# VectorE takes more low parts, the sums of squares end in one buffer, and norms, residual scaling and top-k rounds change places in a three-layer fp32 kernel

## The reference, cut to what matters

```python
def first_block(x, ...):
    x = x + _gla_mixer(_rmsnorm(x, gla_norm), ...)   # head norms, silu(z), w_out
    x = x + _s5_mixer(_rmsnorm(x, s5_norm), ...)
    return _rmsnorm(x, final_norm)

def _s5_mixer(h, ...):
    u, z = jnp.split(h @ w_in, [D_INNER], axis=-1)
    # b_bar from lam, dt and b; states by an associative scan; y = Re(states c) + d_skip * u
    y = jax.nn.gelu(y)
    y = y * jax.nn.sigmoid(y @ w_glu + b_glu) * jax.nn.silu(z)
    return y @ w_out

def second_block(x, meta_tokens, ...):
    h = h + hybrid_mixer(rmsnorm(h, attn_norm_g), pos, topk, ...)
    h = h + swiglu(rmsnorm(h, ffn_norm_g), ...)
    return rmsnorm(h, final_norm_g)[:, N_META:t]

# in hybrid_mixer, for blocks of 128 queries (topk = 128):
    logits = einsum('bqhd,bkd->bqhk', q_idx, k_idx) * idx_scale
    score = einsum('bqh,bqhk->bqk', w_idx, relu(logits))     # index scores
    _, sel = lax.top_k(where(causal, score, -inf), topk)     # then attention over the chosen keys
```

## Time and profile before

| | |
|---|---|
| median of 3 runs | 1885.07 us (1885.0 to 1887.94) |
| the profiled execution's own time | 1887.52 us |
| its span | 1885.7 us |
| mean granted TensorE clock | 0.957 |
| TensorE busy | 1752.2 us, 93% |
| VectorE busy | 1011.8 us, 54% |
| ScalarE busy | 689.3 us, 37% |
| GpSimd busy | 640.9 us, 34% |

### The profile page before, as it was taken

The page is one execution under the profiler, slowest core; times in us unless marked ns, Lnnn a source line. Parts: engine busy times, 40 slices in busy tenths (PEclk is TensorE's granted clock), DMA queues, the critical chain, the costliest instruction groups (busy, mean ns, idle before and its releaser), DMA issues.

```text
span 1885.7 us, 22105 instructions
## 1 busy us (share of the span) xinstructions
PE 1752.2 (93%) x8796; PEld 1419.1 (75%) x8796; DVE 1011.8 (54%) x1469; ACT 689.3 (37%) x1040; POOL 640.9 (34%) x227
## 2 busy tenths in 40 slices
PE   4999999999699999898999999998798999999997
PEld 4777677888588888787788877686576878888786
DVE  4046345486678888897365446599853222222001
ACT  4372225433333353534433331423465322232121
POOL 2433002344522222231134423051574344333441
PEclk8999998999899999799999999899899999999998
DMA  4322001333445544354655322121000333332331
GB/s 136 100 69 80 30 5 63 90 89 101 138 106 144 138 123 122 78 134 111 212 195 168 90 66 67 45 62 56 23 1 23 90 89 90 90 102 79 92 93 60
DMA packets 270941, 172.07 MB, mean 91 GB/s; under 512 B 90971, under 2 KB 249782, under 8 KB 270710
## 3 DMA queue, kind: packets, MB, share of 16 engines
q1 hardware_dynamic: 242272, 146.99, 27.7%
q10 hardware_dynamic: 28262, 22.02, 3.9%
q0 software_dynamic: 304, 1.65, 0.3%
HBM read 149.64 MB, written 20.97 MB: 90 GB/s over the span
## 4 chain that ended last, share of the span: by engine, by line
PE 76%; DVE 11%; ACT 5%; DMA 3%; issue 2%; POOL 1%; ACTq 1%; SPq 0%; DVEq 0%; POOLq 0%
PE PS L680 20%; PE PS L682 20%; PE PS L681 20%; DVE acc L2299 2%; PE PA L932 1%; PE PA L931 1%; POOL ring_lo L2426 1%; PE PA L911 1%; DVE top L2298 1%; PE PA L864 1%; PE PS L1202 1%; PE PA L861 1%; PE PS L1190 1%; PE PA L840 1%; DMA ring<-in_s_w_in 1%
## 5 line engine op out<-in xcount | busy, mean ns | idle before, releaser
L2426 POOL TENSOR_TENSOR ring_lo<-ring,ring_hi 128x2048 fp32r<-128x2048 f32 (+4 forms) x102 | 447.6, 4388 | 909.4 <-ACT ring_hi L1305 908.9
L1305 ACT ACTIVATE ring_hi<-ring 128x2048 fp32r<-128x2048 f32 (+2 forms) x123 | 223.8, 1822 | 213.4 <-PE PS L682 163.8
L680 PE MATMUL PS<-U3h,ring_hi 128*128 128x512 f32 x352 | 140.7, 400 | 3.1 <-POOL ring_lo L2426 3.1
L682 PE MATMUL PS<-U3h,ring_lo 128*128 128x512 f32 x352 | 140.0, 398 | 0.0
L681 PE MATMUL PS<-U3l,ring_hi 128*128 128x512 f32 x352 | 138.6, 394 | 0.0
L2464 POOL TENSOR_TENSOR W<-PW,CZ 128x1024 f32<-128x1024 f32 x16 | 34.6, 2160 | 255.6 <-ACT CZ L1482 255.5
L680 PE MATMUL PS<-HT5h,ring_hi 128*128 128x512 f32 x256 | 108.5, 424 | 0.0
L2391 DVE TENSOR_TENSOR SF<-PS,rs 128x512 f32<-128x512 f32 x22 | 15.2, 692 | 166.7 <-PE PS L682 166.6
L681 PE MATMUL PS<-HT5l,ring_hi 128*128 128x512 f32 x256 | 103.3, 403 | 0.0
L682 PE MATMUL PS<-HT5h,ring_lo 128*128 128x512 f32 x256 | 102.9, 402 | 0.0
L2479 POOL TENSOR_SCALAR PB<-PB,mx 128x144 f32<-128x144 f32 (+3 forms) x64 | 71.2, 1125 | 36.2 <-DVE mx L2348 36.2
...
## 6 DMA issues: line engine op xcount, KB each, us to landing
...
```

What stands on the lines that cost most here:

```text
L680: pe.matmul(dst, w[0], x[0], start=start, stop=False)
L682: return pe.matmul(dst, w[1], x[0], start=False, stop=stop)
L1305: act.activation(ring_hi[:, n % NSLOT, 0:plan.size[n]], ring[:, n % NSLOT, 0:plan.size[n]], ACT.Copy)\
L2426: pool.tensor_tensor(ring_lo[:, n % NSLOT, at], ring[:, n % NSLOT, at], ring_hi[:, n % NSLOT, at].bitcast(F32), ALU.subtract).then_inc(wlo ...
```

## The change: what it does

1. VectorE makes the low parts of four more weight loads: the second and third of the S5 stage, and the first two of the second glu half (`DVE_LOADS`).
2. VectorE also adds the last square of a wide norm to `ssq`, and TensorE sums from `ssq` alone.
3. The head norms' sums stand behind one gate tile and their rows behind the next (`HEAD_SUMS`, `HEAD_USE`).
4. At the start of S5 the reciprocal stands before the last step of `b_factors(0)`, `turns(0)` behind the first scaled u tile.
5. In a batch, `c_to_columns` and `columns` stand behind the second transposes of b.
6. The gelus of batch 13 stand in batch 15.
7. The residual scaling stands in pairs 23 to 30.
8. The low parts of the latent queries stand behind all three scalings; one index score stands a step later.
9. Between the rotations there are 32 top-k rounds instead of 40, in the pairs 24 instead of 16.

```diff
@@ -227,8 +227,8 @@
     LOWS = [range(s5_used[b - 1] + 3 if b else S5_LOAD + 3, s5_used[b] + 3) for b in range(NBATCH)]
-    DVE_LOADS = range(LOWS[0].start, LOWS[-1].stop)
-    assert DVE_LOADS.stop <= S5_END
+    DVE_LOADS = range(S5_LOAD + 1, S5_END + 2)
+    assert LOWS[-1].stop <= S5_END
     pairs("s5_glu", wg2[:, GA:], 0, KI)
@@ -576,6 +576,7 @@
         FIRST_MLA = PAIRS.index(("mla", 0, 0))
+        XT_PAIR = len(PAIRS) - KD - 1
@@ -607,7 +608,7 @@
-            return sum(NORMS[other][2] - 2 for other in WIDE[:WIDE.index(name)]) + max(i, 1)
+            return sum(NORMS[other][2] - 1 for other in WIDE[:WIDE.index(name)]) + max(i, 1)
@@ -646,7 +647,10 @@
-        HEAD_WITH = {0: 0, 2: 1, 6: 2, 10: 3}
+
+
+        HEAD_SUMS = {1: 0, 3: 1, 6: 2, 10: 3}
+        HEAD_USE = {0: 0, 4: 1, 8: 2, 12: 3}
@@ -759,15 +763,9 @@
                     norm_applied(pe, BEFORE[name])
-                parts = [sq[:, (s0 + i) % 2, :] for i in range(k)]
-                if name in WIDE:
-                    pe.wait_ge(squares_summed, summed(name, k - 2))
-                    parts = [ssq, parts[-1]]
-                pe.wait_ge(sq_ready, s0 + k)
+                pe.wait_ge(squares_summed, summed(name, k - 1))
                 for j, w in token_tiles(width):
-                    for i, part in enumerate(parts):
-                        m = pe.matmul(PA[0:w, 3, j:j + 1], part[:, j * P:j * P + w], con[:, C_ONE:C_ONE + 1],
-                                      start=i == 0, stop=i == len(parts) - 1)
+                    m = pe.matmul(PA[0:w, 3, j:j + 1], ssq[:, j * P:j * P + w], con[:, C_ONE:C_ONE + 1], start=True, stop=True)
                 m.then_inc(sq_used, k)
@@ -866,8 +864,13 @@
-            pair_stage("gla_z", lambda k: both((HT2h, HT2l), slice(None), k), split="gla2",
-                       then=lambda i: norm(f"head{HEAD_WITH[i]}", T) if i in HEAD_WITH else None)
+            def head_norms(i):
+                if i in HEAD_SUMS:
+                    norm_sums(f"head{HEAD_SUMS[i]}", T)
+                if i - 1 in HEAD_SUMS:
+                    norm_rows(f"head{HEAD_SUMS[i - 1]}", T)
+
+            pair_stage("gla_z", lambda k: both((HT2h, HT2l), slice(None), k), split="gla2", then=head_norms)
             single_stage("gla_out", lambda k: both((Oh, Ol), slice(None), k), split="o")
@@ -948,19 +951,16 @@
                 beside = BESIDE[b]
+                dense(*beside[0], 0, 1)
+                additions(b)
+                dense(*beside[0], 1, 4)
+                if b + 1 < NBATCH:
+                    b_to_rows(b + 1, 0)
+                dense(*beside[0], 4, KD)
+                if b + 1 < NBATCH:
+                    b_to_rows(b + 1, 1)
                 if b + 2 < NBATCH:
                     c_to_columns(b + 2)
-                if beside[0]:
-                    dense(*beside[0], 0, 1)
-                additions(b)
-                if beside[0]:
-                    dense(*beside[0], 1, 4)
-                if b + 1 < NBATCH:
-                    b_to_rows(b + 1, 0)
-                if beside[0]:
-                    dense(*beside[0], 4, KD)
-                if b + 1 < NBATCH:
-                    b_to_rows(b + 1, 1)
                 if len(beside) > 1:
...
@@ -1416,14 +1411,17 @@
             for i, tile in enumerate(tiles["gla_z"]):
-                if i in HEAD_WITH:
-                    h = HEAD_WITH[i]
-                    norm(f"head{h}", lambda k: O[:, 4 * h + k, :], T, GDV)
+                if i + 1 in HEAD_SUMS:
+                    h = HEAD_SUMS[i + 1]
+                    for k in range(4):
+                        square(f"head{h}", k, O[:, 4 * h + k, :], T)
                 split_weights(tile.loads[-1] + 1)
                 if i >= 2:
                     act.wait_ge(val_ready, VALS["o"] + i - 1)
                 act.wait_ge(tile_done, tile.t + 1)
                 act.activation(SZ[:, i % 2, :], PS[:, 2 * tile.slot, :], ACT.Silu).then_inc(slot_free[tile.slot], 1)
+                if i in HEAD_SUMS:
+                    std(f"head{HEAD_SUMS[i]}", T, GDV)
                 if i > 0:
@@ -1541,18 +1539,19 @@
                         tile_out(stage, m)
-                if b + 2 < NBATCH:
-                    columns(b + 2)
                 split_weights(s5_used[b] + 2)
                 if b + 1 < NBATCH:
                     b_rows(b + 1, 0)
                 tile_out(*BESIDE[b][0])
                 if b + 1 < NBATCH:
                     b_rows(b + 1, 1)
+                if b + 2 < NBATCH:
+                    columns(b + 2)
+                if b + 1 < NBATCH:
                     rotations_of(b + 1)
                     masked(b + 1)
-                if b in (6, 9, 13):
-                    for i in {6: range(4), 9: range(4, 8), 13: range(8, 12)}[b]:
+                if b in (6, 9, 15):
+                    for i in {6: range(4), 9: range(4, 8), 15: range(8, 12)}[b]:
                         gelu(i)
@@ -1681,7 +1680,7 @@
                     high_normed("cq", lambda i: CQh[:, i, :])
-                    high_normed("ckv", lambda i: CKh[:, 0:T2], T2)
+                    high("ckv", 0, ssq[:, 0:T2], CKh[:, 0:T2])
             for i, tile in enumerate(tiles["ks"]):
@@ -1781,7 +1780,7 @@
                 s0, _, k = NORMS[name]
-                if 0 < i < k - 1:
+                if i > 0:
                     dve.wait_ge(sq_ready, s0 + i + 1)
@@ -1948,10 +1947,11 @@
             for i, tile in enumerate(tiles["gla_z"]):
-                if i in HEAD_WITH:
-                    h = HEAD_WITH[i]
+                if i + 1 in HEAD_SUMS:
                     for k in range(4):
-                        sum_squares(f"head{h}", k)
+                        sum_squares(f"head{HEAD_SUMS[i + 1]}", k)
+                if i in HEAD_USE:
+                    h = HEAD_USE[i]
                     norm(f"head{h}", lambda k: O[:, 4 * h + k, :], lambda k: O[:, 4 * h + k, :], PV_HG, T)
...
@@ -2029,7 +2030,7 @@
-            def b_factors(b):
+            def b_factors(b, last=lambda: None):
@@ -2039,6 +2040,7 @@
                 link(tt(four(b_tmp[:]), factor(3, b), rows(BZ[:, p, 1]), ALU.mult))
+                last()
                 tt(Bn[p][:], Bn[p][:], b_tmp[:], ALU.add).then_inc(bf_ready, 1)
@@ -2090,14 +2092,15 @@
             link(dve.memset(dk[:].rearrange("p g n -> p (g n)"), 0.0))
-            b_factors(0)
-            turns(0)
-            inverse_std("s5", T)
+            b_factors(0, lambda: inverse_std("s5", T))
+            low_weights(S5_LOAD + 1)
             dve.wait_ge(rs_ps, NORMS["s5"][1] + 1)
             dve.tensor_copy(sn(rs5[:]), by_block(scale_rows(T))).then_inc(rs5_used, 1)
             dve.wait_ge(rs5_used, 1)
             scaled("s5_u", 0)
+            turns(0)
             scaled("s5_u", 1)
+            low_weights(S5_LOAD + 2)
             b_factors(1)
@@ -2127,6 +2130,8 @@
                 low("g", i, U[:, i, :], *fresh(i))
+            low_weights(S5_END)
+            low_weights(S5_END + 1)
             for i, tile in enumerate(tiles["s5_glu"]):
...
@@ -2196,6 +2199,7 @@
             fin_low(KD - 1)
+            fin_squares(KD - 1)
             dve.memset(CKh[:, T2:TPAD].bitcast(F32), 0.0).then_inc(pad_zero, 1)
@@ -2252,9 +2256,6 @@
             rotate(1)
-            for k in range(KD):
-                stt(out=XT[:, k, :], in0=XT[:, k, :], scalar=pv[:, PV_FIN + k:PV_FIN + k + 1], in1=rs1[:], op0=ALU.mult, op1=ALU.mult)\
-                    .then_inc(normed, 1)
             dve.wait_ge(ki_copied, 1)
@@ -2315,13 +2316,18 @@
             dve.wait_ge(rs_ps, NORMS["ck"][1] + 1)
-            norm_split("cq", lambda k: CQ[:, k, :], lambda k: CQh[:, k, :], lambda k: CQl[:, k, :], PV_GQ, T, CK_PARTS["cq"][2]())
-            dve.wait_ge(xlo_ready, sum(SPLITS["cq"]))
-            norm_split("ckv", lambda k: CK[:], lambda k: CKh[:, 0:T2], lambda k: CKl[:, 0:T2], PV_GKV, T2, CK_PARTS["ckv"][2]())
+            for k in range(2):
+                stt(out=sq[:, k, 0:T], in0=CQ[:, k, :], scalar=pv[:, PV_GQ + k:PV_GQ + k + 1], in1=CK_PARTS["cq"][2](),
+                    op0=ALU.mult, op1=ALU.mult).then_inc(val_ready, 1)
+            stt(out=ssq[:, 0:T2], in0=CK[:], scalar=pv[:, PV_GKV:PV_GKV + 1], in1=CK_PARTS["ckv"][2](),
+                op0=ALU.mult, op1=ALU.mult).then_inc(val_ready, 1)
+            for k in range(2):
+                low("cq", k, sq[:, k, 0:T], CQh[:, k, :], CQl[:, k, :])
+            low("ckv", 0, ssq[:, 0:T2], CKh[:, 0:T2], CKl[:, 0:T2])
             for n in range(12, len(INDEX)):
                 summed_up(n)
                 select(1)
-            for n, rounds in zip(range(FIRST_QS, len(ROTATIONS)), (5, 5, 5, 5, 5, 5, 5, 4, 1, 0, 0)):
+            for n, rounds in zip(range(FIRST_QS, len(ROTATIONS)), (5, 5, 4, 4, 4, 4, 3, 2, 1, 0, 0)):
                 rotate(n)
...
@@ -2360,9 +2365,14 @@
                                              mx[:, n % 6, 0:1]).then_inc(reduced, 1)
-                if 0 < p <= TOPK // 8:
+                if 0 < p <= 3 * TOPK // 16:
                     select(1)
```

(7 more changed lines are left out.)

24 lines of the change are left out of this document (9 added, 15 removed).

## The result

The changed kernel takes 1855.32 us (median of 4 runs, 1852.3 to 1860.15), the kernel before 1885.03. The ratio is 0.9846, with a 95% interval of 0.9818 to 0.9874: 29.7 us less. The prediction was 1848 within 1826 to 1872. The profiled execution took 1852.3 (span 1850.5) where the one before took 1887.52, a difference of 35.2, against −37 in the sum of the prediction. By the medians the sum was 7 us too large, and several of its terms were further off than that and made up for each other.

A forecast was written before the change was run, and what follows sets the result against it. TensorE, busy 93% of the span, was taken as the bound, its matmuls the floor. Terms summed to −37 us, 1887.52 to 1850.5; the median lying 2.45 below the profiled execution gave 1848, range 1826 to 1872.

The forecast's parts named there:

- B: Head norms over two gate tiles: heads 2 and 3 lose sum time and a small wait; −2 us (−8 to +3).
- I: Pairs take over top-k rounds and residual scaling: a third of the rounds and 1 us for scaling, +5 us (0 to +12).
- A: One buffer for norms' sums of squares: half the one-column matmuls go, some clock returns; −6 us (−8 to −4).
- C: Start of S5: waits for the reciprocal and at the transposes of c go, against new costs; −10 us (−15 to −5).
- D: Batches: moved columns, transposes and gelus shorten scans and remove waits, against VectorE held up elsewhere; −4 us (−12 to +3).
- E: Low parts of the first two glu loads by VectorE: a third of one TensorE wait goes; −1 us (−3 to 0).
- F: Residual scaling leaves the rotations: the 4.1 wait for KR goes and 2.8 of clock returns; −7 us (−8 to −5).
- G: Latent queries, scalings before low parts and one index score later: touches the wait at RL; −2.5 us (−4 to −1).
- H: Eight top-k rounds fewer between the rotations, where VectorE sets the pace: −9.5 us (−15 to −5).
- +6: Start of S5: cost of VectorE's two low parts, two PSUM slots and later turns, sine and first scan; +6 us.
- R1: Rival, slower: shared access makes VectorE bound the batches, 3 us more each, 1900; decides from 2.1 per batch; chance 0.05.
- R2: Rival: lateness moves into the pairs, all rounds and eight scalings at 1.76 on the path, 1869 us; chance 0.12.

The follow-up runs named there:

- the first experiment: The changed kernel measured and profiled again with no edit: 1858.22 us, ratio 0.985 to the kernel before.
- doubled sums: Changed kernel with head norms' sums and rows behind one tile again, plus each one-column matmul of the four head sums issued twice: 1850.35 us, ratio 0.9813.
- part 5 alone: Changed kernel with only the transposes of c and ScalarE's columns back at the start of a batch: 1851.51 us, ratio 0.9814 to the kernel before.
- the last kernel of the experiments: Changed kernel with columns back at batch start, heads 2 and 3 still spread, VectorE's part of their norms at tiles 7 and 11: 1838.59 us, ratio 0.9754.

## Why the prediction was right, term by term

The forecast of 1848 within 1826 to 1872 holds the 1855.32, and the direction and most of the mechanisms are as worked out. That the sum came so near is in part luck: B was 5 us too hopeful and I 6 too dear, and they cancel. Each measured number is the difference of two profiles, with the spread of the stretches given at the first experiment.

| term | predicted | measured | how |
|---|---|---|---|
| A, gla, s5 and ffn norms | −1.5 | not measured apart | |
| B, head norms | −2 | +3.3 (+7.4 in the second profile) | 113.9 to 117.2 (121.3) |
| B, of it one buffer | in it | −6.8 | 113.9 to 107.1; +7.7 with doubled sums |
| B, of it spreading | in it | +10 | 107.1 to 117.2 (121.3) |
| C, S5 start | −10 | −7.9 | 47.7 to 39.8 |
| D, without the gelus | 0 | about −0.5 | −4.8 in all less −4.3; part 5 alone +5 to +7 |
| D, gelus | −4 | −4.3 | undone alone |
| E | −1 | −1.2 | second glu half to the first projection |
| A at the final norm, F, G | −13.8 | −13.7 | projections; F alone −6.7 |
| H | −9.5 | −8.7 | 34.1 to 25.3 |
| I | +5 | −1.1 | pairs |

**A** was under-sized by its clock. For a head norm's sums the prediction took 0.85, counted it for two heads in B, and left the clock of all four to B's bound of −8. The four head sums gave 7.7, of which 3.4 are the matmuls themselves. At the final norm the 5.26 of the earlier trace rows became 2.05 for 20 records, less than half, and the 6.8 us at clock 0.52 behind them are gone altogether, where half was taken. The wider norms paid something that the term had at 0.7: with the last addition on VectorE's path TensorE waits 5.9 instead of 4.7 for the sums of the gla norm and 2.5 instead of 1.6 for those of the last one, 1.2 and 0.9 more. The window behind the final norm's sums in after:

```profile
1111.76:1118.56 6.80, 6.80 (x38) 5.72 (x38) 1.41 (x10) 5.39 (x8) 2.72 (x1) 1.00 0.16 46
```

**B** failed at the step "the small wait between sums and rows, since three products of a gate tile now stand between them". There are three products for TensorE, but on VectorE the reciprocal was moved behind something that ends with TensorE's own next tile. I had looked at what moved on TensorE and ScalarE, and not read VectorE's list behind the sums. Heads 0 and 1 also wait 2.6 at 295.5 for the sum, where 1.2 stood, and 3.5 for a low part at 300.9, where nothing stood. In the gate tiles the kernel with VectorE's part one tile earlier and the last kernel of the experiments differ by the order of these two heads alone, 108.1 against 105.1; with one profile each, the 3 us are not told from the spread.

**C** came near its number by another way. The wait of 13.4 went, and the new waits of 4.05 and 3.86 are the "+6". But the place of the reciprocal, the reason stated, is only one of two: the 5.50 of b_tmp and the 4.87 of the turn, which the prediction took as they were, stood beside GpSimd's low parts, and moving these away halves the wait alone. Undoing the order alone cost nothing in the time. The 3.18 at the transposes is gone in after, but it is also gone with the transposes back ahead of the additions (no such wait in the run with the columns back, whose start takes 41.5), so their place is not what closed it; what did is open.

**D** got its sum right by two errors that met, a cost of the new victims that was more than the 4.5 taken and a gain in the clock of which only 2 were counted. The conflict of VectorE and GpSimd behaved as R1 had it: VectorE's busy time in ten batches rose by 24.1 us, 2.4 per batch, above the 2.1 from which R1 was to decide. It did not make the kernel slower, because in the three-tile batches VectorE had idle time for it: 24.4 us before the first product of the scan and 20.2 before the evictions of dense tiles, of which 17.5 and 7.4 were left. Where it had none, before UAl, it cost 6.8 in one piece. The price of R1 was in VectorE's time and not in TensorE's. What made up for it is open in part: with the columns back the two stretches are 11.4 us shorter than before, 4.3 of it by the gelus. The other 7 go with the clock, 0.98 in the batches against 0.95, and the low-clock spots that before has at 518 and 716 are at full clock now; which edit did that no run tells apart.

**F** came as worked out, and its method serves elsewhere: a wait of TensorE, what stood ahead of the awaited instruction, its length, and half of the busy time in the slow window behind. **G** was not undone alone; the waits at RL went from 3.5 to 2.2 in all, about half of its term. **H** had the wait of 4.6 at `ro` right, which is gone. The 4.9 of idle time beside it was read from 1324.1 to 1341.2, and the pairs begin at 1328.5: only 2.8 of it stand before them. What closed beside the 4.6 is the wait for Vm (4.4 to 1.7) and 1.2 of busy time, most of it clock (0.88 to 0.93), which H did not count.

**I** was too dear: the rounds are hidden altogether, and the scaling too. VectorE is busy 26.5 of 31.0 us in the pairs of the third query tile, a share of 0.85 where 0.88 was foretold, and the pairs are no longer for it. An XT operation took 0.73 beside GpSimd's scaling of PB, not 1.76:

```profile
1388.64 0.73 DVE L2374 SCALAR_TENSOR_TENSOR XT<-XT,pv,rs 128x512 f32<-128x512 f32 x1
```

```profile
1388.09 3.18 POOL L2490 TENSOR_SCALAR PB<-PB,mx 128x528 f32<-128x528 f32 x2 [0.83 <-DVE mx L2353]
```

The 1.76 was never the length of one: the 14.05 of the earlier trace rows are six operations of 0.74 and two of 5.1, and these two stood beside GpSimd's low parts (4.79 and 4.97 us). One of them in before:

```profile
1149.34 5.08 DVE L2256 SCALAR_TENSOR_TENSOR XT<-XT,pv,rs 128x512 f32<-128x512 f32 x1
```

So R2, as far as it rested on that conflict, had no ground. The rule that the prediction cites from the Trainium skill, "SBUF — State Buffer", section "Who interferes with whom", was too wide here: GpSimd reads SBUF in both cases, but only its operations with two tensor operands (W, low parts) held VectorE's two-input ones up; all eight XT operations of after, each beside the scaling of PB, took 0.73.

The profiled executions differ by 35.2 and the medians by 29.7: before's profile lay 2.5 above its median, after's 3.0 below. The 1848 took the first into account and could not know the second. The second profile of the changed kernel, at 1857.78, lies 29.7 below before's.
